# Second one-hots of the dense expert gates: all made 512 wide on VectorE and gated on GpSimd, with the stage's low parts of weights moved to VectorE

## The reference, cut to what matters

```python
eid = first_key * 128 + second_key          # by top_k over sums of scores
gate = softmax(best_s, axis=-1)
u = take(expert_down, eid); act = gelu(einsum('thkd,td->thk', u, x))
v = take(expert_up, eid);   out = einsum('thk,thkd->td', gate * act, v)
```

## Time and profile before

| | |
|---|---|
| median of 3 runs | 3469.89 us (3468.11 to 3470.27) |
| span of the profiled execution | 3468.2 us |
| TensorE busy (PE) | 3209.6 us, 93% |
| VectorE busy (DVE) | 1800.2 us, 52% |
| ScalarE busy (ACT) | 1083.1 us, 31% |
| GpSimd busy (POOL) | 490.7 us, 14% |
| the stage of the change | about 743 to 1006 us of the span |

### The profile page before, as it was taken

One profiled execution on the slowest core, in us unless ns is written; L12 is line 12 of the kernel. 1 busy time (PEld: TensorE's weight loads), 2 busy tenths in 40 slices (PEclk: granted clock), 3 DMA queues, 4 the chain that ended last, 5 costly groups with the idle time before them and its releaser, 6 DMA issues. The chain is left out here.

```text
span 3468.2 us, 40822 instructions
## 1 busy us (share of the span) xinstructions
PE 3209.6 (93%) x14684; PEld 2506.8 (72%) x14684; DVE 1800.2 (52%) x3019; ACT 1083.1 (31%) x1540; POOL 490.7 (14%) x296
## 2 busy tenths in 40 slices
PE   8868999988889999999999999979898899989998
PEld 6622778876677888788888886658776778668886
DVE  4452449979955555444444445543224445444444
ACT  3152322233334334222222224231113233442223
POOL 0100005544442222000000000223220000000000
PEclk9985999999999999999999999979789999999999
DMA  4200224435455554333333332200002223122222
GB/s 140 70 0 11 101 74 137 137 116 199 184 194 211 180 180 167 106 118 121 118 118 117 119 117 93 67 9 1 1 1 85 85 88 130 38 82 95 92 95 73
DMA packets 105603, 352.93 MB, mean 102 GB/s; under 512 B 10241, under 2 KB 11137, under 8 KB 103970
## 3 DMA queue, kind: packets, MB, share of 16 engines
q1 hardware_dynamic: 105506, 351.65, 30.0%
HBM read 299.18 MB, written 52.43 MB: 101 GB/s over the span
## 5 line engine op out<-in xcount | busy, mean ns | idle before, releaser
L129 ACT ACTIVATE weights_hi<-weights_raw 128x1024 fp32r<-128x1024 f32 x459 | 478.2, 1052 | 774.3 <-PE psum L146 371.0
L160 PE MATMUL psum<-act_hi,weights_hi 128*128 128x512 f32 x1368 | 546.8, 400 | 31.8 <-DVE act_lo L348 15.6
L137 DVE TENSOR_TENSOR weights_lo<-weights_raw,weights_hi 128x1024 fp32r<-128x1024 f32 x399 | 502.4, 1267 | 88.0 <-ACT weights_hi L129 86.8
L160 PE MATMUL psum<-act_lo,weights_hi 128*128 128x512 f32 x1368 | 544.2, 398 | 0.0
L160 PE MATMUL psum<-act_hi,weights_lo 128*128 128x512 f32 x1368 | 543.7, 397 | 0.0
L146 PE MATMUL psum<-inner_hi,weights_hi 128*128 128x512 f32 x1280 | 506.4, 396 | 2.1 <-DVE inner_lo L1491 2.1
L146 PE MATMUL psum<-inner_hi,weights_lo 128*128 128x512 f32 x1280 | 505.6, 395 | 0.0
L146 PE MATMUL psum<-inner_lo,weights_hi 128*128 128x512 f32 x1280 | 505.6, 395 | 0.0
L160 PEld LDWEIGHTS psum<-act_hi,weights_hi 128*128 128x128 f32 x1368 | 259.2, 189 | 101.3 <-issue 36.3
L160 PEld LDWEIGHTS psum<-act_hi,weights_lo 128*128 128x128 f32 x1368 | 259.3, 190 | 63.1
L160 PEld LDWEIGHTS psum<-act_lo,weights_hi 128*128 128x128 f32 x1368 | 259.4, 190 | 62.2 <-issue 0.5
(11 more groups left out here) (351 smaller groups left out, 4628.1 us busy)
## 6 DMA issues: line engine op xcount, KB each, us to landing
weights_raw<-in_u_experts SPq DMA_DIRECT2D x256, 512.0 KB, 3.6
gates_dram<-gates_stage SPq DMA_DIRECT2D x8, 4096.0 KB, 12.2
gates_of_group<-gates_dram SPq DMA_DIRECT2D x16, 2048.0 KB, 11.3
weights_raw<-in_u_mlp SPq DMA_DIRECT2D x64, 512.0 KB, 3.5
ups_dram<-up_products SPq DMA_DIRECT2D x64, 256.0 KB, 2.2
up_group<-ups_dram SPq DMA_DIRECT2D x8, 2048.0 KB, 8.9
weights_raw<-in_u_in SPq DMA_DIRECT2D x24, 512.0 KB, 3.6
weights_raw<-in_u_merge SPq DMA_DIRECT2D x24, 512.0 KB, 3.6
```

The costliest lines, as they stand in the source:

```text
L129: self.nc.scalar.activation(self.hi[slot][:, :, :], self.raw[:, slot, :].rearrange("p (c n) -> p c n", c=C), ACT.Copy).then_inc(self.hi_re ...
L137: eng.tensor_tensor(self.lo[slot][:, :, :], self.raw[:, slot, :].rearrange("p (c n) -> p c n", c=C), self.hi[slot][:, :, :].bitcast(F32), ...
L160: mm = self.nc.tensor.matmul(out, w[slot][:, c, :], a[:, j, 0:tokens], start=first and n == 1, stop=last and n == 3 * len(chunks))
```

## The change

All second one-hots become one 512-column comparison on VectorE, and all are gated by GpSimd. The signal `hot2_ready` goes, TensorE waits for `hot2_gated` in every step. VectorE's loop has the same 32 steps as the others' and now makes the low parts, behind the third step of each unit, and those of the tail.

```diff
             @block.vector
             def _(dve):
-                with dve.Fori(0, T // QUAD // HOTS) as i:
-                    for k in range(HOTS):
-                        dve.wait_ge(dense_ready.sem, i * HOTS + (k + 1))
-                        one_hots(hot1[k], 0, i, k).then_inc(hot1_ready.sem, 1)
-                        if k % 2:
-                            one_hots(hot2[k], 1, i, k).then_inc(hot2_raw.sem, 1)
-                            continue
-                        for t in range(QUAD):
-                            token = i * (HOTS * QUAD) + (k * QUAD + t)
-                            ins = nc.vector.tensor_scalar(hot2[k][:, t, :], iota[:, :], picks_t[:, 1, bass.ds(token, 1)], picks_t[:, 2, bass.ds(token, 1)],
-                                                          ALU.is_equal, ALU.mult)
-                        ins.then_inc(hot2_ready.sem, 1)
+                with dve.Fori(0, T // LOOP_TOKENS) as i:
+                    for n in range(LOOP_STEPS):
+                        dve.wait_ge(dense_ready.sem, i * LOOP_STEPS + (n + 1))
+                        one_hots(hot1[n % HOTS], 0, i, n).then_inc(hot1_ready.sem, 1)
+                        one_hots(hot2[n % HOTS], 1, i, n).then_inc(hot2_raw.sem, 1)
+                        if n % C == 2:
+                            weights.lo_step(dve, i, n // C + weights.AHEAD, LOOP_UNITS)
+                for k in tail:
+                    weights.lo_step(dve, None, k + weights.AHEAD, None)

             @block.gpsimd
             def _(pool):
                 with pool.Fori(0, T // LOOP_TOKENS) as i:
-                    for u in range(LOOP_UNITS):
-                        for n in range(u * C // 2, (u + 1) * C // 2):
-                            if n == u * C // 2 + 1:
-                                weights.lo_step(pool, i, u + weights.AHEAD, LOOP_UNITS)
-                            pool.wait_ge(hot2_raw.sem, i * (LOOP_STEPS // 2) + (n + 1))
-                            hot = hot2[(2 * n + 1) % HOTS]
-                            nc.gpsimd.tensor_tensor(hot[:, :, :], hot[:, :, :],
-                                                    picks_t[:, 2, bass.ds(i * LOOP_TOKENS + (2 * n + 1) * QUAD, QUAD)].unsqueeze(2).to_broadcast([P, QUAD, P]),
-                                                    ALU.mult).then_inc(hot2_gated.sem, 1)
-                for k in tail:
-                    weights.lo_step(pool, None, k + weights.AHEAD, None)
+                    for n in range(LOOP_STEPS):
+                        pool.wait_ge(hot2_raw.sem, i * LOOP_STEPS + (n + 1))
+                        hot = hot2[n % HOTS]
+                        nc.gpsimd.tensor_tensor(hot[:, :, :], hot[:, :, :],
+                                                picks_t[:, 2, bass.ds(i * LOOP_TOKENS + n * QUAD, QUAD)].unsqueeze(2).to_broadcast([P, QUAD, P]),
+                                                ALU.mult).then_inc(hot2_gated.sem, 1)
...
                             pe.wait_ge(hot1_ready.sem, i * LOOP_STEPS + (n + 1))
-                            gated_hots = hot2_gated if k else hot2_ready
-                            pe.wait_ge(gated_hots.sem, i * (LOOP_STEPS // 2) + (n // 2 + 1))
+                            pe.wait_ge(hot2_gated.sem, i * LOOP_STEPS + (n + 1))
                             pe.wait_ge(dense_copied.sem, i * LOOP_STEPS + (n + 1))
```

More of the change, by code:

```diff
@@ L1140, in build_program @@
             return
-        hot1_ready, hot2_ready, dense_ready, dense_copied = (sig(n) for n in ("first_one_hots_ready", "gated_one_hots_ready", "dense_gates_ready", "dense_gates_copied"))
-        hot2_raw, hot2_gated = sig("odd_second_one_hots_ready"), sig("odd_second_one_hots_gated")
+        hot1_ready, dense_ready, dense_copied = (sig(n) for n in ("first_one_hots_ready", "dense_gates_ready", "dense_gates_copied"))
+        hot2_raw, hot2_gated = sig("second_one_hots_ready"), sig("second_one_hots_gated")
         gates_stored = [sig(f"gates_stored{k}") for k in range(2)]
@@ L1166, in _, with one_hots @@
             def _(dve):
-                def one_hots(hot, r, i, k):
+                def one_hots(hot, r, i, n):
                     return nc.vector.tensor_tensor(hot[:, :, :], iota[:, :].unsqueeze(1).to_broadcast([P, QUAD, P]),
-                                                   picks_t[:, r, bass.ds(i * (HOTS * QUAD) + k * QUAD, QUAD)].unsqueeze(2).to_broadcast([P, QUAD, P]),
+                                                   picks_t[:, r, bass.ds(i * LOOP_TOKENS + n * QUAD, QUAD)].unsqueeze(2).to_broadcast([P, QUAD, P]),
                                                    ALU.is_equal)
-                with dve.Fori(0, T // QUAD // HOTS) as i:
-                    for k in range(HOTS):
-                        dve.wait_ge(dense_ready.sem, i * HOTS + (k + 1))
-                        one_hots(hot1[k], 0, i, k).then_inc(hot1_ready.sem, 1)
-                        if k % 2:
-                            one_hots(hot2[k], 1, i, k).then_inc(hot2_raw.sem, 1)
-                            continue
-                        for t in range(QUAD):
-                            token = i * (HOTS * QUAD) + (k * QUAD + t)
-                            ins = nc.vector.tensor_scalar(hot2[k][:, t, :], iota[:, :], picks_t[:, 1, bass.ds(token, 1)], picks_t[:, 2, bass.ds(token, 1)],
-                                                          ALU.is_equal, ALU.mult)
-                        ins.then_inc(hot2_ready.sem, 1)
+                with dve.Fori(0, T // LOOP_TOKENS) as i:
[7 more added lines that the diff above has]
+                    weights.lo_step(dve, None, k + weights.AHEAD, None)
             @block.gpsimd
```

## The result

The changed kernel takes 3488.24 us (median of 4 runs, 3487.31 to 3490.35) against 3470.08 us (4 runs, 3468.11 to 3470.91): 18.2 us slower, ratio 1.0052, 95% interval 1.0038 to 1.0066. The forecast was 3489.1 us. The profiled span is 3486.4 us against 3468.2.

A forecast was written before the change was run, and what follows sets the result against it. The prediction took VectorE to bound the stage: its stream grows from 260.5 to 279.7 us, so 3468.2 + 19.2 = 3487.4 us of span. With the runs' median 1.7 above the span, the forecast was 3489.1 us, range 3482 to 3499.

The forecast's parts named there:

- VectorE bounds the stage: Stretch 743 to 1006 us: VectorE, busy 260.45 of 263.00 us, sets the stage's end and the TensorE work behind it.
- The stream: VectorE's instructions in the changed stage: 1.20 + 260.4 + 18.1 + 0.08 = 279.7 us, against 260.5 before.
- (a): Second one-hots in 64 steps: four narrow instructions, 1.03 us, become one wide at 0.60; 27 us less.
- (b): Wide one-hots beside gatings in the new loop: one free spacing and one blocked, 0.60 + 1.45 = 2.05 us a step.
- The lower bound: Wide one-hots in the new loop: L1168 isn't held by GpSimd at all, a step of 0.60 + 0.60 us.
- rival B: Every second one-hots of the stage: wide ones aren't held by GpSimd, TensorE binds with 205 us, 3414 us; chance 0.05.
- (c): Stage's 16 low parts moved from GpSimd to VectorE: 32.8 us of VectorE's time go, 18.1 come.
- The lead over ScalarE's high part: Before VectorE's low parts: high part ready at 3.3 us, asked for at 4.6; lead 1.2 us, priced at nothing.
- (d): TensorE in the stage's loop: one step with nothing to wait for takes 1.60 us, under 2.05.
- What follows is unchanged: Behind the stage: it ends 19.2 us later and the rest keeps its time, giving a span of 3487.4 us.
- the sign that the prediction named for it: Trace after, TensorE in the stage: its idle time in front of L1213 would be released by GpSimd.

The follow-up runs named there:

- no gating: The changed kernel with GpSimd's 128 gatings left out, TensorE waiting for the second one-hots themselves: 3410.62 us, ratio to before 0.9829.
- the row in PSUM: The changed kernel with the row 0 to 127 that all one-hots compare with read from PSUM, all gatings kept: 3426.95 us, ratio 0.9876.
- all narrow: The changed kernel with all second one-hots as four 128-column compare-and-gate instructions on VectorE, no GpSimd in the stage's loop: 3436.65 us, ratio 0.99.
- Half gating: The changed kernel with GpSimd gating only two of the four tokens of each step, 256 of 512 columns: 3436.31 us, ratio 0.9905.
- write only: The changed kernel with each gating replaced by a GpSimd memset of 512 columns behind a 4-column multiplication: 3423.6 us, ratio 0.9863.
- the row in PSUM and late low parts: The changed kernel with the compared row in PSUM and low parts behind the seventh step of each unit instead of the third: 3412.22 us, ratio to before 0.9833.
- low parts alone: The kernel before, in a loop of 32 steps, with only the stage's low parts moved to VectorE: 3453.74 us, ratio 0.9956.

## Why the prediction was right

It was right in direction, mechanism and size: 3489.1 against 3488.24 us, inside 3482 to 3499. By its steps:

- **VectorE bounds the stage.** Shown: in the changed kernel its stream and the span grew together, and the stage shrinks as soon as VectorE is let go (no gating, the row in PSUM), down to TensorE's 1.60 a step. The stream was put at 279.7 us; from its first instruction at 744.35 to the end of its last pair, 1021.88 + 2.13 = 1024.01, it is 279.7.
- **(a) narrow against wide.** 1.03 and 0.60 as stated (all narrow).
- **(b) a wide one held for 0.85.** 1.52 long, one step 2.05, as read off L1584. The lower bound, that broadcast operands aren't held, fell with the first held L1168; the row in PSUM shows what would have had to be different for rival B. Half gating shows that the value belongs to the length of GpSimd's instruction.
- **(c) low parts.** 16.5 us for this part alone, 14.7 stated; in the other direction, put back into the changed kernel, 16.8. The lead over ScalarE's high part was put at 1.2 us; in the trace after (ScalarE's and VectorE's order of time below), a high part ends at 817.67 + 1.05 = 818.72 and VectorE takes it at 819.78, 1.1 us later. In all units of that trace but the first the lead is 0.97 to 1.06. That it goes when the stage gets quicker, and that VectorE then stands there, is what three experiments ran into (no gating, the row in PSUM, write only); only with GpSimd's instructions between VectorE and TensorE did it cost time.
- **(d) TensorE's 1.60** is what binds with no gating and with the row in PSUM and late low parts.
- **Where it was off.** "What follows is unchanged" is right only in the net, and that the forecast came within a microsecond is in part luck. VectorE's first instruction came at 744.35 instead of 743.12, before anything that was changed: +1.2. In the experiments it lay anywhere between 742.7 and 745.8, so this is not put down to the change. Against it, behind the stage 2.2 us were given back. Of these, 1.2 stand behind the change of blocks, where the first 61 matmuls start within 16.8 us before and 15.6 after; the granted clock fits: before it was at 1.2 GHz (0.50) for 5.5 us there, now at 0.59 for 3.3 us and 0.88 for the next 3.0, as the stretches below show. The trace of low parts alone has 15.6 too, so nothing ties this to the change; the cause is left open, and all of it is within the spread of the runs. And of TensorE's idle time in the stage 119 us are put down to "issue" in the view of waits, 25 to VectorE and 6 to GpSimd, in one wait: the sign that the prediction named for it isn't there, though GpSimd's gating is what TensorE's wait asks for.

```profile
817.67 1.05 ACT L129 ACTIVATE weights_hi<-weights_raw 128x1024 fp32r<-128x1024 f32 x1
```
```profile
819.78 1.21 DVE L137 TENSOR_TENSOR weights_lo<-weights_raw,weights_hi 128x1024 fp32r<-128x1024 f32 x1
```
```profile
1052.70:1056.00 3.30, 3.02 (x8) 2.42 (x9) 1.23 (x1) 1.06 (x1) 3.18 (x2) 0.59 0.63 163
1056.00:1059.00 3.00, 3.00 (x13) 2.39 (x12) 0.00 (x0) 0.00 (x0) 3.00 (x4) 0.88 0.96 264
```

The rule of the Trainium skill (SBUF — State Buffer, "Who interferes with whom") held in its finer parts, each now with a run: the wide one-hots are held with two SBUF inputs and not with one (the row in PSUM: 681 ns and no hold), and GpSimd must read (write only: 683 ns and no hold). Its statement that the pair is held for the full instruction isn't what spacing shows: 1.04 us of GpSimd cost VectorE 0.85.

## What to carry to other kernels

Work moved to GpSimd isn't off VectorE while GpSimd reads SBUF and VectorE runs instructions like these, with two tensors in SBUF: price it at its own length less 0.2 us on VectorE's stream (this held for lengths of 0.20, 0.61, 1.04 and 2.4 us), and look for the price in instructions that have become longer, since no wait shows it. If one of VectorE's two inputs is small and constant, a copy in PSUM can free both engines; here that, with the low parts four steps later, turned an 18 us loss into a gain of 58. Once an engine is let go, look again at what it meets first in its own order: a low part asked for four steps too early was worth 15 us.

## What the hardware showed that I hadn't expected

- Alone, GpSimd's multiplication of 4 columns takes 0.20 us, 256 columns of gating 0.61 and 512 columns 1.04: about 0.19 fixed and 1.65 ns for each column. So the fixed 0.2 that a hold lacks has the size of the part that does not grow with the columns. Its memset of 512 columns takes 0.52.
- Where a multiplication of GpSimd had to wait for a VectorE instruction, it ended the same time behind that one, whatever the step: 0.06 us for 4 columns, 0.47 for 256, 0.90 for 512, each 0.14 under its length alone. VectorE's next instruction never took GpSimd's turn.
- The same low part on GpSimd is 2.41 us in the median beside VectorE's narrow instructions and 2.81 beside its wide ones, where it has to wait for the end of one first (11 of the 16 here):

```profile
L137 POOL TENSOR_TENSOR weights_lo<-weights_raw,weights_hi x11: 2798/2805/2812, 751.1 to 936.7; 128x1024 fp32r<-128x1024 f32 x11
```

- One-hots whose row comes from PSUM are as quick as those from SBUF, 681 ns in the median against 679 in the kernel before.
